# Modulation product dealt over four 32-column groups of TensorE, in chunks that alternate with split ones

## The reference

```python
sc = jax.nn.silu(c)                 # c: (1, 2048)
scc = jax.nn.silu(c_ctx)            # c_ctx: (2048,)
xc = ctx
for l in range(DEPTH):              # DEPTH = 2
    shift, scale, gate = jnp.split(sc @ w_ada[l] + b_ada[l], 3, axis=-1)
    shift_c, scale_c, gate_c = jnp.split(scc @ w_ada[l] + b_ada[l], 3, axis=-1)
    h = rms(x, norm_w[l]) * (1.0 + scale[:, None]) + shift[:, None]
    hc = rms(xc, norm_w[l]) * (1.0 + scale_c) + shift_c
    ...                             # u = h @ w_in, three attentions, silu(z) gate
    x = x + gate[:, None] * merge_out(o_a, o_b, o_c, z, w_out[l])
```

## Time and profile before

| | us |
|---|---|
| median of three runs | 4747.82 |
| lowest, highest | 4742.44, 4751.39 |
| the profiled execution, first to last instruction (span) | 4738.1 |

### The profile page before, as it was taken

How to read it: one execution, slowest core, us unless ns; L and a number is a source line. 1 busy time by engine, 2 the same in 40 slices (tenths; PEclk the granted TensorE clock), 3 DMA queues, 4 the chain that set the end, 5 groups by cost and what they waited for, 6 DMA issues and landing times.

```text
span 4738.1 us, 53399 instructions
## 1 busy us (share of the span) xinstructions
PE 4286.8 (90%) x19088; PEld 3160.5 (67%) x19088; DVE 1739.7 (37%) x2641; ACT 1678.4 (35%) x2583; POOL 68.9 (1%) x120
## 2 busy tenths in 40 slices
PE   7899998989899998997988988999679987999998
PEld 1466655667565665775666666777257766999876
DVE  0322213332222224333313444444144445666544
ACT  1221213334312114333344353444234545555433
POOL 3000000000000000000000000000000000000000
PEclk9999995559899999995599999999789998999999
DMA  8444430001144443330014554566035434656564
GB/s 256 141 138 137 134 119 0 1 3 42 48 138 149 137 148 111 111 97 2 0 47 124 181 147 140 162 185 177 0 127 181 150 120 125 186 187 186 175 194 152
DMA packets 350494, 575.97 MB, mean 122 GB/s; under 512 B 25252, under 2 KB 130868, under 8 KB 348208
## 3 DMA queue, kind: packets, MB, share of 16 engines
q1 hardware_dynamic: 344000, 549.39, 37.9%
q0 software_dynamic: 6384, 25.14, 1.8%
HBM read 570.26 MB, written 4.19 MB: 121 GB/s over the span
## 4 chain that ended last, share of the span: by engine, by line
PE 51%; DVE 4%; ACT 4%; issue 2%; DMA 0%; DVEq 0%; ACTq 0%
PE ps L646 31%; PE ps L1199 11%; PE ps L737 2%; PE ps L954 1%; PE ps L728 1%; DVE w_lo L624 1%; PE ps L924 1%; ACT w_hi L618 1%; PE ps L1110 1%; PE ps L1103 1%; PE ps L904 1%; PE ps L824 0%; ACT f_arena L1243 0%; PE ps L665 0%; PE ps L978 0%
## 5 line engine op out<-in xcount | busy, mean ns | idle before, releaser
L624 DVE TENSOR_TENSOR w_lo<-raw_ring,w_hi 128x1024 fp32r<-128x1024 f32 (+1 forms) x827 | 1010.7, 1224 | 1750.2 <-ACT w_hi L618 1738.4
L618 ACT CAST w_hi<-raw_ring 128x1024 fp32r<-128x1024 f32 (+1 forms) x827 | 864.5, 1047 | 1880.6 <-PE ps L646 1407.9
L646 PE MATMUL ps<-w_hi,r_a 128*128 128x512 f32 x3552 | 1280.6, 402 | 87.4 <-DVE w_lo L624 61.8
L646 PE MATMUL ps<-w_lo,r_a 128*128 128x512 f32 x2624 | 1045.0, 398 | 0.0
L646 PE MATMUL ps<-w_hi,r_b 128*128 128x512 f32 x2272 | 865.1, 400 | 14.2 <-DVE w_lo L624 11.9
L646 PEld LDWEIGHTS ps<-w_hi,r_a 128*128 128x128 f32 x3552 | 675.7, 190 | 285.7 <-issue 79.6
L646 PEld LDWEIGHTS ps<-w_lo,r_a 128*128 128x128 f32 x2624 | 499.2, 190 | 116.2
L646 PEld LDWEIGHTS ps<-w_hi,r_b 128*128 128x128 f32 x2272 | 431.6, 190 | 126.7 <-DVE w_lo L624 13.8
L1199 PE MATMUL ps<-r_a,w_hi 128*128 128x256 f32 x2816 | 497.6, 280 | 3.0 <-DVE w_lo L624 3.0
L1199 PEld LDWEIGHTS ps<-r_a,w_hi 128*128 128x128 f32 x2816 | 431.3, 189 | 3.3 <-issue 3.2
L1199 PE MATMUL ps<-r_a,w_lo 128*128 128x256 f32 x1408 | 394.4, 280 | 0.0
(11 more groups left out here) (289 smaller groups left out, 3170.0 us busy)
## 6 DMA issues: line engine op xcount, KB each, us to landing
raw_ring<-in_w_in_dram SPq DMA_DIRECT2D x386, 512.0 KB, 3.7
raw_ring<-in_w_ada_dram SPq DMA_DIRECT2D x192, 512.0 KB, 4.3
raw_ring<-in_ffn_w_up_dram SPq DMA_DIRECT2D x176, 512.0 KB, 3.5
raw_ring<-in_w_out_dram SPq DMA_DIRECT2D x96, 512.0 KB, 4.0
raw_ring<-in_ffn_w_down_dram SPq DMA_DIRECT2D x88, 512.0 KB, 4.6
raw_ring<-in_w_proj_b_dram SPq DMA_DIRECT2D x32, 512.0 KB, 3.9
raw_ring<-in_w_proj_a_dram SPq DMA_DIRECT2D x16, 512.0 KB, 4.1
raw_ring<-in_w_qb_dram SPq DMA_DIRECT2D x24, 288.0 KB, 2.9
```

The costliest lines, as they stand in the source:

```text
L618: nc.scalar.copy(WH[:, ph.s_slot(j), 0:n], RAW[:, ph.raw_slot(j), 0:n]).then_inc(hi_ready, 1)
L624: nc.vector.tensor_tensor(WL[:, ph.s_slot(j), 0:n], RAW[:, ph.raw_slot(j), 0:n], WH[:, ph.s_slot(j), 0:n].bitcast(F32), ALU.subtract).then ...
L646: mm = nc.tensor.matmul(PS[:, ti, 0:cols], X(x, k, t), W[w][:, ph.s_slot(j), kk * cols:(kk + 1) * cols], start=(k == 0 and q == 0), stop=( ...
```

## The change

Column groups: the instruction for k writes partitions 32 (k mod 4) and the next, in bank 7, so four partial sums of four k-tiles each stand at partitions 0, 32, 64 and 96. The row copy takes 98 partitions. The turning matmul contracts over 98 of them with a selector `ada_sel` (98 x 2) that is one at partitions 32g + s and zero elsewhere, and so adds the four partial sums. Bank 7 is cleared once at the start, since the partitions between have to be finite, and the selector is made from the identity; PE waits for both (`ada_clear`).

Alternation: in `win0`, `z0` and `wout0` the chunks of a block come as split, plain, split, plain (`pairs`), for SP's loads as for PE; the split chunks have the even places (`JS[0]`). `win1`, `z1` and `wout1` stay as they were.

```diff
+ADAG = 4
+ADAM = 32 * (ADAG - 1) + 2
...
+        SEL = place("ada_sel", 2)
...
-        ADAR = F[0:2, E0 + 6144:E0 + 6144 + NB]
+        ADAR = F[0:ADAM, E0 + 6144:E0 + 6144 + NB]
...
+        def pairs(a, b):
+            return [c for two in zip(a, b) for c in two]
+
+        JS = (list(range(0, 16, 2)), list(range(8)))
...
-                phase("win0", 8, blk("S", w_in[0], 2, 8) + blk("P", w_ada[1], 2, 8))
+                phase("win0", 8, pairs(blk("S", w_in[0], 2, 8), blk("P", w_ada[1], 2, 8)))
...
-                phase("z0", 4, blk("S", w_in[0], 2, 8, ZC) + blk("P", w_ada[0], 2, 8, blk0=8))
-                phase("wout0", 4, blk("S", A["w_out"][0], 2, 8) + blk("P", w_ada[1], 2, 8, blk0=8))
+                phase("z0", 4, pairs(blk("S", w_in[0], 2, 8, ZC), blk("P", w_ada[0], 2, 8, blk0=8)))
+                phase("wout0", 4, pairs(blk("S", A["w_out"][0], 2, 8), blk("P", w_ada[1], 2, 8, blk0=8)))
...
-                mm = nc.tensor.matmul(PS[0:2, 7, :], SCT[:, k, :], RAW[:, ph.raw_slot(j), kk * NB:(kk + 1) * NB],
-                                      start=(k == 0), stop=(k == KT - 1))
+                g = 32 * (k % ADAG)
+                mm = nc.tensor.matmul(PS[g:g + 2, 7, :], SCT[:, k, :], RAW[:, ph.raw_slot(j), kk * NB:(kk + 1) * NB],
+                                      start=(k < ADAG), stop=(k >= KT - ADAG))
...
-                mm = nc.tensor.matmul(ADAP[:, f, :], ADAR[:, f * P:f * P + P], ident[0:2, 0:2],
+                mm = nc.tensor.matmul(ADAP[:, f, :], ADAR[:, f * P:f * P + P], SEL[0:ADAM],
...
-            nc.vector.tensor_copy(ADAR, PS[0:2, 7, :]).then_inc(ada_row, 1)
+            nc.vector.tensor_copy(ADAR, PS[0:ADAM, 7, :]).then_inc(ada_row, 1)
...
+            pe.wait_ge(ada_clear, 1)
...
                         for c in range(8):
-                            pe_block_part(pe, ph, i, S8, c, 2, NB, x1, range(4), st)
+                            pe_block_part(pe, ph, i, JS[0], c, 2, NB, x1, range(4), st)
                             if c == 1 and not (isinstance(i, int) and i == 0):
                                 pe_ada_turn(pe, ada_n[0] + i - 1)
-                        for c in range(8):
-                            pe_ada(pe, ph, i, 8 + c, c, ada_n[0] + i)
+                            pe_ada(pe, ph, i, 2 * c + 1, c, ada_n[0] + i)
...
-                    gemm_wait(act, st, t, tiles, ph, i, 7)
+                    gemm_wait(act, st, t, tiles, ph, i, JS[l][7])
...
+            V.memset(PS[:, 7, :], 0.0)
+            dve.wait_ge(consts_in, 16)
+            V.tensor_reduce(SEL, ident.rearrange("p (g n) -> p n g", g=4)[:, 0:2, :], AX_X, ALU.add).then_inc(ada_clear, 1)
```

More of the change, by code:

```diff
@@ L409, in build @@
         ss_ready, ms_ready, rt_ready, rinv_ready = sem("ss_ready"), sem("ms_ready"), sem("rt_ready"), sem("rinv_ready")
-        ada_row, ada_tr = sem("ada_row"), sem("ada_tr")
+        ada_row, ada_tr, ada_clear = sem("ada_row"), sem("ada_tr"), sem("ada_clear")
         ada_free, amul_ready, act_link, dve_link = sem("ada_free"), sem("amul_ready"), sem("act_link"), sem("dve_link")
@@ L991, in _ @@
                         for c in range(8):
-                            pe_block_part(pe, ph, b, S8, c, 2, NB, x1, range(T), AC["z0"][b])
+                            pe_block_part(pe, ph, b, JS[0], c, 2, NB, x1, range(T), AC["z0"][b])
                             if c == 1 and b:
                                 pe_ada_turn(pe, ada_n[0] + b - 1)
-                        for c in range(8):
-                            pe_ada(pe, ph, b, 8 + c, c, ada_n[0] + b)
+                            pe_ada(pe, ph, b, 2 * c + 1, c, ada_n[0] + b)
                     else:
@@ L1336, in win_body @@
                     def win_body(i):
-                        for q in S8:
+                        for q in JS[0]:
                             act_hi(act, ph, i, q)
@@ L1437, in z_evac @@
                         a = 16 * l + b * T + t
-                        gemm_wait(act, st, t, T, ph, b, 7)
+                        gemm_wait(act, st, t, T, ph, b, JS[l][7])
                         if a >= 2:
@@ L1442, in _ @@
                 for b in range(4):
-                    for q in S8:
+                    for q in JS[l]:
                         act_hi(act, ph, b, q)
@@ L1454, in _ @@
                         GATEB[:, k // 4, (k % 4) * NB:(k % 4) * NB + NB], b))
-                hi_loop(PH[f"wout{l}"], S8, None)
+                hi_loop(PH[f"wout{l}"], JS[l], None)
             act.wait_ge(acc_free, AC["uv"][0][0])
@@ L1822, in win_body @@
                     def win_body(i):
-                        for q in S8:
-                            dve_lo(dve, ph, i, q)
+                        for q, j in enumerate(JS[0]):
+                            dve_lo(dve, ph, i, j)
                             if not (isinstance(i, int) and i == 0):
@@ L1972, in _ @@
                 for b in range(4):
-                    for q in S8:
-                        dve_lo(dve, ph, b, q)
+                    for q, j in enumerate(JS[l]):
+                        dve_lo(dve, ph, b, j)
                         if l and q == 0 and b:
@@ L2008, in w_evac @@
                     for t in range(T):
-                        gemm_wait(dve, st, t, T, ph, b, 7)
+                        gemm_wait(dve, st, t, T, ph, b, JS[l][7])
                         L(TT(PS[:, t, :], PS[:, t, :], GATEB[:, t // 2, ds(b * NB, NB)], ALU.mult))
@@ L2013, in _ @@
                 if l == 0:
-                    lo_loop(ph, S8, lambda b: dve_ada_row(dve, ph, b, 15), T,
+                    lo_loop(ph, JS[0], lambda b: dve_ada_row(dve, ph, b, 15), T,
                             lambda b: dve_ada_bias(dve, 1, 8 + b, ada_n + b), w_evac)
```

## The result

| | before | after |
|---|---|---|
| median of the runs, us | 4746.36 (4 runs) | 4630.04 (4 runs) |
| lowest, highest | 4742.44, 4751.39 | 4627.09, 4635.07 |
| ratio, 95% interval | | 0.9756, 0.9744 to 0.9768 |
| span of the profiled execution | 4738.1 | 4633.1 |

The change makes the kernel 116 us faster, 2.4%; in the two profiled executions the difference is 105 us (the profiled execution of the changed kernel is the slowest of its four). The forecast was 48 us and the range ended at 4640, 10 us above the median.

A forecast was written before the change was run, and what follows sets the result against it. PE was taken as the bound; the opening -20, win0 -12, z0 -7 and wout0 -9 sum to -48 us, a span of 4690 and a forecast median of 4700 us. The range was 4640 to 4766 us.

The forecast's parts named there:

- The bound and the places: PE bounds the kernel's modulation product in four stretches: the opening, win0, z0 and wout0.
- Records side by side: Plain chunk of two instructions: only second record of k and first of k+1 overlap, 1.28 us a chunk.
- The first rival: Full overlap: each column group has its own order, a chunk takes 0.85 us; -97, 4651 us in all; chance 0.20.
- Changes of shape: Each plain chunk inside a block of win0, z0, wout0 costs 0.27 us for switching into L679 and back.
- the dear case: Rival: half overlap, but a pair of shape changes costs 0.35 us more; +39 on the forecast, 4739 us; chance 0.15.
- The opening: First stretch, 8 blocks: streaming halves, loads become the bound at 308 GB/s, end at 140.9 instead of 161.2; -20 us.
- a fall of the clock and loads below 290 GB/s: Signs of error in the opening: PE falls to 1.2 GHz and binds again, or loads stay below 290 GB/s.
- A term that the sum lacked: Making the selector, a memset and reduction on DVE before the first row copy, was priced at nothing.
- Block ends: In win0 ACT's last-tile copy precedes the next cast: next block starts 3.64 us after plain start, waiting 2.2 us.
- I price nothing: Clock loss at block-end waits priced at zero; slow restarts cost 1.6 us each, 25 at most for sixteen.
- The slower rival: Groups take turns, alternation costs: win0 +12, z0 +5, wout0 +3, opening 0; +20, 4768 us; chance 0.20.
- The rule against the change: Weight loads overlap matmuls in flight only across row groups; column groups share rows, so time would be the second rival's.

The follow-up runs named there:

- e9: The changed kernel with another 32 bytes of unused room, so r_a, f_arena and r_b lie 32 bytes beyond a multiple of 64 again; 4652.85 us.
- e4: The changed kernel with only column group 0 in the opening and four groups behind it; 4635.39 us.
- e2: The changed kernel with one column group instead of four, chunks still alternating; 4720.88 us.
- e3: The changed kernel with two column groups (k mod 2) instead of four; 4633.63 us.
- e6: The changed kernel with chunks in the order split, split, plain, plain, so four instructions in four groups stand together; 4540.31 us.
- e1: The changed kernel with the old chunk order, eight split then eight plain, so column groups alone; 4663.49 us.
- e8: The kernel before with 32 unused bytes where the changed kernel puts its selector, so r_a, f_arena and r_b begin at a multiple of 64; 4706.77 us.
- e10: The changed kernel with one more, filling matmul in each chunk of the opening, into a bank nobody reads; 4630.30 us.

## Why the prediction was wrong

**The bound and the places** held: PE bound the four stretches, and the gain of the groups lies in them.

**Records side by side** is the step that failed. I reasoned that the second record of instruction k holds back instruction k+1, "so it can't begin before that one has streamed, and k+1 stands behind it". Only its first half is so. The trace shows the first records of all instructions at hand beginning 7 ns apart and their second ones a length later. A chunk takes 0.85 us, not 1.28: for the seven inner chunks of 16 blocks that is 48 of the 57 us by which the forecast (48) falls short of the profiles (105). The rows of before, all in one group, could not show an order between groups; I took one group's order for the engine's. The first rival had it right, and its sum for win0, z0 and wout0, 36 + 20 + 21 = 77 us, stands against 36.3 + 19.5 + 22.1 = 77.9 in the profiles. That the match is so close is partly luck: 3072 matmuls at 3.7 ns less give another 11 us there, and eight slow restarts more, at 1.45, take 12 back. That rival's total, 4651 us, lay inside the range; e9, which has the groups, the alternation and the old address, takes 4652.85, again with some luck, since its opening gained less than the 20 us of that sum.

**A term that the sum lacked**: the prediction costs the selector at nothing, since it looked at the two instructions that make it and not at the room it takes. Its 32 bytes move `r_a` and `r_b`, and that is worth 40 us on the kernel before and 23 on the changed one, the 16 us from win1 on among them. It is what takes the changed kernel below the end of the range at 4640, and no rival foresaw a gain outside the changed phases.

**Changes of shape**: 0.27 us for a pair was forecast. A plain chunk costs 1.16 us with them, of which 0.85 is streaming: 0.31. Right, and the dear case did not come.

**The opening**: -20 was forecast, -9.4 came in the profile, and the median of e4 is 5 us above that of the changed kernel, within the noise between sets. The loads did become the bound, but at 287 GB/s and not at 308, with PE at a lower clock. Both were named as what would make the forecast wrong, a fall of the clock and loads below 290 GB/s; both came, but PE did not become the bound. Two of the later kernels with the same instructions in the opening did reach 142 us, with loads at 308 and 311 GB/s, the others 146.7 to 151.2 at 282 to 295: the term was taken from a burst of 4 us, and what the opening gains differs between executions by up to 9 us.

**Block ends**: the mechanism and size were right (ACT's queue, 3.64 forecast, 3.53 measured; waits of 2.5 in win0 instead of 2.2, since the chunk before is shorter). "I price nothing" for the clock was not: 10 slow restarts instead of 2 cost 12 us, half of the 25 that stood as the most. Behind waits up to 1.65 us, all of e2, none of 13 restarts was slow, and in all twelve traces none is slow behind less than 1.90 us. Behind longer ones both happen: at 2.5 us in win0 all seven are slow in the changed kernel, but 5 of 7 in e3, 4 in e9 and 3 in e6, and e1 has fast ones behind 2.98 us. What decides is left open.

**The slower rival** (turns, +20) can be held against e2, which has one group and alternates: 14 us above the kernel before with the same address (4720.88 against 4706.77). In the profiles win0 takes 9.7 us more in e2 than in e8, z0 5.3 more and wout0 2.4 less, where +12, +5 and +3 stood; e8 has three slow restarts in these phases and e2 none, which is 4 us of the difference. So its mechanism was sound for one group. Its condition, that two groups take turns, is refuted.

**The rule against the change**, that a weight load passes matmuls in flight only in another row group (the Trainium skill, TensorE: Matmul & The Clock Gate, Part 3), is refuted for columns: the eight weight loads of four column groups stand between 15.518 and 15.542 us, amid the matmuls of the first ones, in the same rows. PE's weight loads in the changed kernel, cut at 15.6 us:

```profile
15.52 0.11 PEld L687 LDWEIGHTS ps<-raw_ring,silu_c_t 128*2 128x2 f32 x8 [2.38 <-ACT silu_c_t L1298]
```

The Trainium skill's TensorEngine Tiling (Array Packing), section Theoretical Speedup, names up to four times the speed where one small dimension is at most 32. The trace agrees: four float32 instructions in the 0.85 us of one.

## What to carry to other kernels

Products with few stationary columns take a quarter of the time when four neighbours write different column groups and are at hand together (0.85 us for four float32 instructions of 512 columns, where one group took 3.4): give the engine four in a row, not two, since two and four cost the same here. When work that hid a hand-over at a block's end is shrunk or moved, move the next block's first step ahead of the evacuation in every queue; here this was worth as much as a third of the change. And when a change adds a tile, look at where the others move to, before a gain or loss in untouched phases is put down to the change itself.

## What the runs showed of the hardware

- Float32 matmuls in four column groups of 32 begin 7 ns apart and run four at a time (eight records in 1.04 us, e6); the order of records holds within a group alone, and an instruction of another group passes one that waits in its own (101.83 against 102.24 us, e10).
- Fp32r matmuls with 128 x 128 stationary operands and 512 columns follow each other every 229.4 to 229.7 ns when `r_a` and `r_b` begin at a multiple of 64 bytes in the partition (ten kernels), every 233.3 to 233.4 ns when they lie 32 bytes off (two). Over this kernel 0.9%, from one unused gap of 32 bytes (e8).
- With several groups at work PE's clock was granted at 0.72 to 0.94 in the opening, where PE was 68 to 73% busy, and at 1.00 where the same work took turns and kept PE 95% busy; the same instructions got different clocks in different executions.
